# A state space scan in one long Trainium2 kernel: decays from spread running sums in the short format

## The reference, as far as it matters

```
a_cs  = cumsum(dt * A)                              # running sums, 128 tokens
decay[l, s] = exp(a_cs[l] - a_cs[s]) for l >= s, else 0
y_diag[l]   = sum_s (C[l] . B[s]) * decay[l, s] * x[s] * dt[s]
state_new   = state * exp(a_cs[last]) + sum_l B[l] * exp(a_cs[last] - a_cs[l]) * x[l] * dt[l]
y_off[l]    = (C[l] . state) * exp(a_cs[l])
y = (y_diag + y_off + d_skip * x) * silu(z)
```

## Time and profile before

| what | us |
|---|---|
| median of three runs | 2659.7 |
| span of the profiled execution | 2655.9 |
| TensorE busy | 2315.8 |
| vector engine busy | 1566.5 |
| GpSimd busy | 1499.5 |
| ScalarE busy | 716.4 |

### The profile page before, as it was taken

The page is one execution under the profiler, slowest core; times in us unless marked ns, Lnnn a source line. Parts: engine busy times, 40 slices in busy tenths (PEclk is TensorE's granted clock), DMA queues, the critical chain, the costliest instruction groups (busy, mean ns, idle before and its releaser), DMA issues.

```text
span 2655.9 us, 28354 instructions
## 1 busy us (share of the span) xinstructions
PE 2315.8 (87%) x9216; PEld 1516.6 (57%) x9216; DVE 1566.5 (59%) x3390; ACT 716.4 (27%) x1940; POOL 1499.5 (56%) x1060
## 2 busy tenths in 40 slices
PE   8999999999999999698889888898777777777776
PEld 7888778788878879586754444443233222222222
DVE  1266791434430678622388888887788776555555
ACT  2111552215421240523232222212223222111112
POOL 6777477676467763373655655655544454334331
PEclk9999999999999999899999999999999999999999
DMA  4222002222322210031399999999999999999996
GB/s 148 88 100 97 16 15 90 96 96 81 104 80 95 95 48 1 9 111 40 120 378 421 421 421 421 420 415 420 421 422 422 421 421 422 421 422 421 422 421 253
DMA packets 105898, 646.35 MB, mean 243 GB/s; under 512 B 12720, under 2 KB 15152, under 8 KB 39600
## 3 DMA queue, kind: packets, MB, share of 16 engines
q0 software_dynamic: 73728, 536.90, 48.7%
q1 hardware_dynamic: 31776, 106.87, 11.7%
q10 hardware_dynamic: 272, 1.05, 0.1%
HBM read 640.58 MB, written 4.19 MB: 243 GB/s over the span
## 4 chain that ended last, share of the span: by engine, by line
DMA 32%; PE 11%; DVE 5%; POOL 2%; issue 1%; ACT 1%; POOLq 0%; DVEq 0%; ACTq 0%
DMA peer_row<-in_peer_uv,peer_ids 32%; PE bank L3332 8%; DVE peer_row L3277 2%; PE bank L2837 1%; PE bank L2997 1%; POOL peer_row L3254 1%; ACT peer_diag L3311 1%; DVE peer_weight L3269 1%; POOL w_parts L232 1%; POOL w_parts L228 0%; PE bank L2959 0%; DVE peer_top_i L2681 0%; DVE peer_place L2681 0%; DVE peer_sc_left L2684 0%; DVE peer_top_v L2677 0%
## 5 line engine op out<-in xcount | busy, mean ns | idle before, releaser
L3332 PE MATMUL bank<-peer_row,peer_diag 128*128 128x512 f32 x2048 | 968.6, 619 | 256.9 <-ACT peer_diag L3311 255.5
L3254 POOL DMA_INDIRECT peer_row<-in_peer_uv,peer_ids x512 | 584.9, 1142 | 650.7 <-PE bank L3332 613.2
L3332 PEld LDWEIGHTS bank<-peer_row,peer_diag 128*128 128x128 f32 x2048 | 382.0, 195 | 812.5 <-ACT peer_diag L3311 416.0
L3277 DVE CUSTOM_DVE_ANT_0 peer_row<-peer_row,peer_h_tok 128x1024 f32<-128x1024 f32 x512 | 646.1, 1267 | 327.5 <-DMA peer_row<-in_peer_uv,peer_ids 326.8
L209 POOL TENSOR_TENSOR w_parts<-ring,zero 128x1024 fp32r<-128x1024 f32 x148 | 280.2, 1893 | 193.3 <-PE bank L260 84.4
L212 POOL TENSOR_TENSOR w_parts<-ring,w_parts 128x1024 fp32r<-128x1024 f32 x148 | 354.4, 2395 | 27.7 <-POOL w_parts L209 27.7
L3315 ACT ACTIVATE peer_acts<-peer_dots 128x2 f32<-128x2 f32 x256 | 52.1, 203 | 740.5 <-DVE peer_dots L3277 740.4
L3311 ACT ACTIVATE peer_diag<-ident,peer_weight 128x128 f32<-128x128 f32 x512 | 177.4, 394 | 220.7 <-DVE peer_weight L3269 220.4
L260 PE MATMUL bank<-ssm_h_high,w_parts 128*128 128x512 f32 x512 | 158.0, 389 | 0.8 <-DVEq L645 0.8
L260 PEld LDWEIGHTS bank<-ssm_h_high,w_parts 128*128 128x128 f32 x512 | 96.1, 188 | 21.1 <-DVEq L645 1.0
L284 PE MATMUL bank<-w_parts,att_h_high 128*128 128x512 f32 x320 | 98.8, 390 | 1.6 <-DVE att_h_low L445 1.6
(11 more groups left out here) (571 smaller groups left out, 3815.3 us busy)
## 6 DMA issues: line engine op xcount, KB each, us to landing
ring<-in_weights SPq DMA_DIRECT2D x180, 512.0 KB, 3.2
peer_row<-in_peer_uv,peer_ids POOLq DMA_INDIRECT x512, 24.2
resid<-in_x SPq DMA_DIRECT2D x4, 512.0 KB, 6.2
out<-resid SPq DMA_DIRECT2D x4, 512.0 KB, 7.8
xa_mem<-in_mem ACTq DMA_DIRECT2D x1, 1024.0 KB, 5.0
xa_kept<-xa_v_out SPq DMA_DIRECT2D x1, 1024.0 KB, 6.0
xa_kept<-xa_k_out SPq DMA_DIRECT2D x1, 1024.0 KB, 3.8
xa_v<-xa_kept SPq DMA_DIRECT2D x1, 1024.0 KB, 4.8
```

Source lines behind the costliest of these rows:

```text
L3254: pool.indirect_dma_start(self.rows[row][:, :], None, self.m.ins["peer_uv"], bass.IndirectOffsetOnAxis(ap=self.choice.ids[:, t, slot:slot ...
L3277: dot = dve.tensor_tensor_reduce(mine, mine, self.tokens(slot_of(j)[0]), 1.0, 0.0, ALU.mult, ALU.add, self.dots[:, h % 4, r:r + 1])
L3332: mm = pe.matmul(self.m.banks[2 * t + half][:, :], self.diag[:, j % (2 * GROUP), :], self.rows[row][:, D + half * 512:D + (half + 1) * 512 ...
```

## The change

The exponent a_cs[l] - a_cs[s] is now made from running sums that have been computed once. In the first block the sums of all heads are copied twice side by side (`twice`), transposed to rows (64 partitions: 32 heads twice, bank 7), and split into a high part in the short format F32R and the remainder (`halves`). GpSimd spreads them: row (h) holds the sums of head h in the column block h mod 4 and zero in the others (`spread_sums`). A 64 x 128 selection matrix per group (`chosen`) then sums high and low of the right heads. In the scan, TensorE adds two F32R matmuls into one bank (always bank 0): a unit matrix times the mask (`not_yet`, 0 or -2^100), and `chosen` times `spread_sums`. ScalarE takes four exponentials out of the bank with -a_cs[s] as a bias column, into SBUF. The cuts and the mask product on the vector engine are gone; `mix` multiplies the decays from SBUF with the C·B product out of its bank. y now lags by two units on TensorE and by three on the vector engine; x * dt and x * dt_end go round a ring of eight units; the banks are dealt out anew. The spreads of chunks 0 and 1 are in the first block, those of 2 and 3 in the scan's GpSimd queue at units 1 and 3.

```diff
+spread_sums = m.at(conved_kb, "ssm_sum_spread", [2 * HEADS, TT, HPG, P], F32R)
+chosen = m.at(conved_kb + 8, "ssm_chosen", [2 * HEADS, GROUPS, P], F32R)
+halves = sb("ssm_sum_halves", [2 * HEADS, TT, P], F32R)
...
+eye = sb("ssm_eye", [P, P], F32R)
+not_yet = sb("ssm_not_yet", [P, HPG, P], F32R)
...
+NEVER = -(2.0 ** 100)
+
+def spread_sum(pool, ch):
+
+    return pool.tensor_tensor(spread_sums[:, ch, :, :], again(halves[:, ch, :], HPG), spread(of_residue[:, :], P), ALU.mult)
...
-    SUMS_AFTER, EXPS_AFTER = 13, 15
-    turn_banks = [m.banks[n] for n in (0, 1, 2, 3, 5, 6, 7)]
+    SUMS_AFTER, EXPS_AFTER, SUMS_TURN_AFTER = 13, 15, 15
+    turn_banks = [m.banks[n] for n in (0, 1, 2, 3, 5, 6)]
+    sums_bank = m.banks[7]
...
+            if j == SUMS_TURN_AFTER:
+                pe.wait_ge(twice_made, 1)
+                for t in range(TT):
+                    mm = pe.transpose(sums_bank[0:2 * HEADS, t * P:(t + 1) * P],
+                                      twice[:, t, :, :].rearrange("p x h -> p (x h)"), m.ident[:, :])
+                mm.then_inc(sums_turned, 1)
+
+    @block.gpsimd
+    def _(pool):
+        pool.tensor_copy(eye[:, :], m.ident[:, :])
+        pool.tensor_scalar(not_yet[:, :, :], again(m.after[:, :], HPG), NEVER, None, ALU.mult)
+        pool.wait_ge(masks_made, 1)
+        pool.wait_ge(turned, TT + 2)
+        pool.tensor_copy(chosen[:, :, :], spread(of_group[:, 2, :], P))
+        pool.wait_ge(halves_made, 1)
+        for ch in range(2):
+            spread_sum(pool, ch)
...
+        dve.tensor_reduce(of_residue[:, :], ident.rearrange("p (m r) -> p r m", r=HPG), AX.X, ALU.add)
+        step(dve.tensor_reduce(of_group[:, 0:2, :].rearrange("p x g -> p (x g)"), ident.rearrange("p (n r) -> p n r", r=HPG),
+                               AX.X, ALU.add))
+        dve.tensor_tensor(of_group[:, 2, :], of_group[:, 0, :], of_group[:, 1, :], ALU.add).then_inc(masks_made, 1)
...
-        copies(7, N_TURN - 4)
+        copies(7, 13)
+        dve.wait_ge(pe_dt, 1)
+        sums = m.banks[4][:, 0:P].rearrange("p (t o h) -> p t o h", t=TT, o=1).broadcast_to([P, TT, 2, HEADS])
+        dve.tensor_copy(twice[:, :, :, :], sums).then_inc(twice_made, 1)
+        copies(13, 17)
+        dve.wait_ge(sums_turned, 1)
+        dve.tensor_copy(halves[:, :, :].rearrange("p t l -> p (t l)"), sums_bank[0:2 * HEADS, :]).then_inc(high_made, 1)
+        copies(17, 19)
+        low = halves[HEADS:, :, :].rearrange("p t l -> p (t l)")
+        dve.wait_ge(high_made, 1)
+        dve.tensor_tensor(low, sums_bank[HEADS:2 * HEADS, :], low, ALU.subtract).then_inc(halves_made, 1)
+        copies(19, N_TURN - 4)
...
-        act.wait_ge(pe_dt, 1)
+        act.wait_ge(twice_made, 1)
...
-        act.activation(tmp[:, 1, :], m.banks[4][:, 0:P], ACT.Copy).then_inc(act_dt, 1)
+        act.activation(flat(sum_neg), m.banks[4][:, 0:P], ACT.Copy, scale=-1.0).then_inc(act_dt, 1)
...
-x_dt = conved[:, 0:8, :].rearrange("p (b a) n -> p b (a n)", b=2)
-x_end = conved[:, 8:16, :].rearrange("p (b a) n -> p b (a n)", b=2)
-cut = sb("ssm_cut", [P, 2, HPG, P])
-cb_low = sb("ssm_cb_low", [P, 2, P])
+RING_X = GROUPS
+x_dt, x_end = (conved[:, n:n + 4, :].rearrange("p a n -> p (a n)").rearrange("p (u w) -> p u w", w=GW) for n in (8, 12))
+decay = sb("ssm_decay", [P, 2, HPG, P])
...
-LEAD = 2
+LEAD = 3
+Y_LAG, FINAL_LAG = 2, 3
...
+    seg_bank = m.banks[0]
+    cb_bank = lambda i: m.banks[1 + i % 2][:, 0:P]
+    y_bank = lambda i: m.banks[3 + i % 3][:, 0:GW]
+    new_bank = lambda i: m.banks[3 + i % 3][:, GW:]
+    old_bank = lambda i: m.banks[6 + i % 2][:, 0:GW]
...
-            if ch >= 2:
-                pool.wait_ge(y_done, i - 2 * GROUPS + 1)
+            if i >= RING_X:
+                pool.wait_ge(y_done, i - RING_X + 1)
...
         for i in range(N):
             if i + LEAD < N:
                 prepare(i + LEAD)
+            if i in (1, 3):
+                spread_sum(pool, 2 + i // 2).then_inc(spread_ready, 1)
             fade_state(i)
...
-        for i in range(N + 1):
+        for i in range(N + Y_LAG):
             if i < N:
                 ch, g = units[i]
-                pe.wait_ge(cut_ready, i + 1)
+                if i >= 1:
+                    pe.wait_ge(decay_ready, i)
+                if g == 0 and ch >= 2:
+                    pe.wait_ge(spread_ready, ch - 1)
+
+                pe.matmul(seg_bank[:, :], eye[:, :], not_yet[:, :, :].rearrange("p r l -> p (r l)"), start=True, stop=False)
+                pe.matmul(seg_bank[:, :], chosen[:, g, :], spread_sums[:, ch, :, :].rearrange("p r l -> p (r l)"),
+                          start=False, stop=True).then_inc(seg_done, 1)
+                at = slice(ch * P, (ch + 1) * P)
                 if i >= 2:
                     pe.wait_ge(mix_ready, i - 1)
...
+                pe.matmul(cb_bank(i), b_tiles[:, g, at], c_tiles[:, g, at], start=True, stop=True).then_inc(cb_done, 1)
+            if i >= Y_LAG:
+                j = i - Y_LAG
                 ch, g = units[j]
                 at = slice(ch * P, (ch + 1) * P)
...
                 pe.wait_ge(mix_ready, j + 1)
                 pe.wait_ge(x_ready, 2 * j + 2)
...
+                if j >= 3:
+                    pe.wait_ge(y_read, j - 2)
+                    pe.wait_ge(state_ready, j - 2)
+                if ch > 0:
+                    pe.wait_ge(state_ready, j - GROUPS + 1)
                 for r in range(HPG):
...
+                    pe.matmul(y_bank(j)[:, r * HD:(r + 1) * HD], mix[:, j % 2, r, :],
+                              x_dt[:, j % RING_X, r * HD:(r + 1) * HD], start=True, stop=True)
                 if ch > 0:
 
-                    pe.matmul(yb[:, GW:2 * GW], c_tiles[:, g, at], state[:, g, :], start=True, stop=True)
-                pe.matmul(sbk[:, 0:GW], b_tok[:, ch, g * STATE:(g + 1) * STATE],
-                          x_end[:, ch % 2, g * GW:(g + 1) * GW], start=True, stop=True).then_inc(y_done, 1)
+                    if j >= GROUPS + 2:
+                        pe.wait_ge(old_weighed, j - GROUPS - 1)
+                    pe.matmul(old_bank(j), c_tiles[:, g, at], state[:, g, :], start=True, stop=True)
+                pe.matmul(new_bank(j), b_tok[:, ch, g * STATE:(g + 1) * STATE], x_end[:, j % RING_X, :],
+                          start=True, stop=True).then_inc(y_done, 1)
...
+            if i < N:
+                ch, g = units[i]
+                act.wait_ge(seg_done, i + 1)
+                if i >= 2:
+                    act.wait_ge(mix_ready, i - 1)
+                for r in range(HPG):
+                    h = g * HPG + r
+                    last = act.activation(decay[:, i % 2, r, :], seg_bank[:, r * P:(r + 1) * P], ACT.Exp,
+                                          bias=sum_neg[:, ch, h:h + 1])
+                last.then_inc(decay_ready, 1)
...
+        for i in range(N + FINAL_LAG):
+            f = i - FINAL_LAG
+            if f >= 0:
+                ch, g = units[f]
+                y = y_bank(f)
+                dve.wait_ge(y_done, f + 1)
+                if ch > 0:
+                    dve.tensor_tensor(heads(part[:, f % 2, :]), heads(old_bank(f)), per_head(group(grow[:, ch, :], g), HPG), ALU.mult)\
+                       .then_inc(old_weighed, 1)
+                dve.wait_ge(skip_ready, f + 1)
+                dve.tensor_tensor(y, y, xs[:, ch, wide(g)], ALU.add).then_inc(skip_added, 1)
             if i < N:
+                dve.wait_ge(decay_ready, i + 1)
                 dve.wait_ge(cb_done, i + 1)
-                step(dve.tensor_tensor(cb_low[:, i % 2, :], m.banks[2 + i % 2][:, 0:P], m.upto[:, :], ALU.mult))
-                dve.wait_ge(decay_ready, i + 1)
                 if i >= 2:
                     dve.wait_ge(y_done, i - 1)
-                dve.tensor_tensor(mix[:, i % 2, :, :], m.banks[i % 2][:, :].rearrange("p (h l) -> p h l", h=HPG),
...
+                dve.tensor_tensor(mix[:, i % 2, :, :], decay[:, i % 2, :, :], again(cb_bank(i), HPG), ALU.mult).then_inc(mix_ready, 1)
+            if f >= 0:
+                dve.wait_ge(skip_added, f + 1)
                 if ch > 0:
-                    dve.tensor_tensor(heads(old), heads(yb[:, GW:2 * GW]), per_head(group(grow[:, ch, :], g), HPG), ALU.mult)\
-                       .then_inc(old_weighed, 1)
...
+                    dve.wait_ge(old_weighed, f - GROUPS + 1)
+                    dve.tensor_tensor(y, y, part[:, f % 2, :], ALU.add).then_inc(old_added, 1)
...
-                    dve.tensor_copy(state[:, g, :], sbk[:, 0:GW]).then_inc(state_ready, 1)
+                    dve.tensor_copy(state[:, g, :], new_bank(f)).then_inc(state_ready, 1)
...
+                    dve.wait_ge(faded, f - GROUPS + 1)
+                    dve.tensor_tensor(state[:, g, :], state[:, g, :], new_bank(f), ALU.add).then_inc(state_ready, 1)
+                    dve.wait_ge(old_added, f - GROUPS + 1)
                 gated = z_gate[:, ch, wide(g)]
                 dve.tensor_tensor(gated, gated, y, ALU.mult).then_inc(y_read, 1)
-        m.keep(step)
```

(58 more changed lines are left out.)

27 lines of the change are left out of this document (9 added, 18 removed).

## The result

The changed kernel has a median of **2684.93 us** in four runs (2683.58 to 2689.79) against 2660.61 for the kernel before in the same comparison (2659.52 to 2666.25, four runs). The ratio is 1.0089, with a 95% interval from 1.0072 to 1.0107. The forecast was 2649.2 and its range ended at 2655.5: the forecast had the wrong sign and was off by 36 us.

The account below looks back on a forecast made before the run. TensorE was taken to set the scan's pace at 2.84 us per unit. Scan -11.9, block before +1.4 and clock 0 gave 2645.4; plus 3.8 from profiled span to median, 2649.2 us, range 2646.0 to 2655.5.

Parts of the forecast that it names:

- 0.86 becomes 0.44: Decay sums on TensorE in each scan unit: two short-format matmuls at 0.22 each, 0.42 us less per unit.
- at worst the 0.43 of today: Upper bound for each of the two short-format decay-sum matmuls on TensorE, expected at 0.22 us each.
- rival F: Decay sums in the scan: the short-format pair still runs at 0.43 each, unit stays 2.84, time 2661.4 us; chance 0.02.
- Clock. I take 0, with -0.5 to +1.5 as bounds: TensorE's idle gap after the scan grows to about 4 us; half clock already paid, so no cost.
- a head of 4.34: Scan's start until first y: first units run at the pace of the ScalarE loop, y lags by two; 4.34 us.
- Rival D: Scan and block before: handshakes cost more and the clock falls in the head's gaps; +5.8, 2655 us; chance 0.09.
- The last step: After the scan: what follows starts when its last instruction ends, so a microsecond saved there is one saved overall.
- The block before: Block of transposes ahead of the scan: added work, ending with GpSimd's spreads, costs +1.4 us, bounds 0 and +2.8.
- ScalarE: four exponentials: Each scan unit: four 128-wide exponentials with a bias column, read from the bank, take 1.14 us.
- The tail: Scan's end on the vector engine, three units behind: 7.4 us, with finals 29, 30 and 31 at 1.82 each.
- Rival E: Scan: the vector product reading decays from SBUF blocks GpSimd, whose unit becomes 3.09; +9.3, 2669 us; chance 0.05.
- Rival B: Later scan chunks: GpSimd takes over the pace, its unit 2.53 if the fade waits; 2652 us; chance 0.13.

Follow-up runs that it names:

- variant 6: variant 4 with the sums' matmul reading only 64 of its 128 rows and a second such matmul right behind it: 2674.33 us, ratio 1.0052.
- variant 2: The changed kernel with TensorE's pauses ahead of and inside the scan's head filled by matmuls whose result nobody reads: 2663.63 us, ratio 1.0017.
- variant 1: The changed kernel with the decay sums laid out over 128 partitions instead of 64, the selection's upper rows zero: 2654.32 us, ratio 0.9982.
- variant 4: The changed kernel with both the sums over 128 partitions and TensorE's pauses filled: 2651.90 us, ratio 0.9971.
- variant 10: variant 4 with chunk 1's spread moved from the first block to GpSimd's queue in the scan: 2653.54 us, ratio 0.9981.
- variants 3: The changed kernel with one more full-format 256-column matmul, result not read, in each first-chunk unit: 2677.77 us, ratio 1.0073.
- variant 8: The changed kernel with only the pause ahead of the scan shortened by two full-format matmuls: 2683.05 us, ratio 1.0088.
- variant 7: The changed kernel with only the pauses between the scan's first units filled, by four short matmuls each: 2670.50 us.

## Why the prediction was wrong

**The decay sums, "0.86 becomes 0.44": the first step that failed.** "The contraction of the second is over 64 partitions; the columns count, so I take no less time" was half right: the load of 64 rows takes 0.18 where 128 take 0.19, and a matmul more of this kind adds 0.23 (variant 6). What was missing is the change of row count before and behind it, 0.39 per unit; the time of 0.44 became 0.83. The upper bound "at worst the 0.43 of today" was the truth, by another mechanism than rival F's, which had 0.02; F's time, 2661.4, is near what variant 2 gives with the clock held (2663.6). The row that I priced with, 90 matmuls in 20 us, holds only matmuls over 128 partitions and could not show it. Over the scan this is 8 x (2.40 - 1.94) + 21 x (2.83 - 2.42) = 12.3 us.

**"Clock. I take 0, with -0.5 to +1.5 as bounds": the second, and beside the first the dearer.** I looked at the gap after the scan and not at its head. My own sum had the warning in it: three times 0.66 of TensorE's work in a head of 4.34, behind a block whose end waits 2 us for GpSimd's spreads. Rival D named it, "the clock falls in the longer gaps of the head", and priced it at 1.5; it cost: in the head, (305.56 - 302.81) - (302.81 - 300.69) = 0.6 and about 0.9 more to the first y (2.03 from 305.56 to 307.59, against 1.18 in variant 2); 8 x (4.43 - 2.40) = 16.2; 1.8 in the ninth unit. Together 19.5. Most of this is not the clock's alone. The two errors met: in variant 1 the clock fell just the same, but with all loads covered it was back in 7 us (303.1 to 309.9), and its fall cost some 3 us instead of 19. Had the step on the sums been right, the change would have come out at about 2654, inside the range, with the error in the clock hidden in it. Why the uncovered loads kept the clock down for so long isn't shown.

The scan's length, by steps, from its first matmul to its last instruction's end (head to first y, units, tail):

| | forecast | changed kernel | variant 4 |
|---|---|---|---|
| head | 4.34 | 6.90 | 4.69 |
| units of first chunk | 8 x 1.94 | 8 x 4.43 | 8 x 2.01 |
| 21 later units | 50.82 | 61.28 | 51.39 |
| last units and tail | 9.16 | 9.11 | 9.11 |
| scan | 79.8 | 112.8 | 81.3 |

Once both causes are taken away, in variant 4, the sum of the scan stands to within 1.5 us. The last step held there too: the next block begins 7.9 us earlier than before, and the median is 7.0 lower. Point by point, in the changed kernel:

- The block before: its end came at 300.69 - 299.11 = **1.6** later, forecast 1.4; GpSimd's two spreads of 1.03 set it, nearly as said. They end at 299.99, and the vector engine's last product, of 128x128 with both operands in SBUF, at 300.14: beside a spread it took 0.83, and 0.28 before the change and in variant 10, where no spread runs beside it. The sum had no such wait.
- ScalarE: four exponentials in **1.14**, as the earlier trace rows had it.
- The tail: the finals alone are 1.79 apart (forecast 1.82), TensorE stands still for 3.49 after the scan (forecast about 4).
- Rival E, GpSimd blocked by the product: it holds **0.61** next to it. E falls, for a product with one operand in a bank; two engines do get in each other's way where both operands lie in SBUF, as the line on the block before shows.
- Rival B, GpSimd's pace: at 2.45 per unit in variants 1 and 4, the windows have it busy 19.37 of 20.00 against the vector engine's 19.27. It was near, but TensorE still set the pace.
- What was to show it wrong, a distance above 2.5 between the small matmuls, did.

## What to carry to other kernels

A matmul over fewer partitions than its neighbours isn't free because its columns are few: look whether its weight load, and the next one's, starts under the matmul before or with its own. Where it doesn't, padding to the neighbours' rows with zero weights is faster; here 0.39 us per unit.

A change that makes TensorE's work shorter and leaves it waiting for another engine between bursts must be priced at both clocks: first the pauses at the head of a stage, then how long the clock stays down behind them; it was 44, 10 and 7 us in three versions of the same chunk (the changed kernel, variants 3 and 1). The busy column doesn't tell it (34.00 of 34.00 at 0.50); the granted clock does. Ten matmuls whose result nobody reads, placed in the pauses, were worth 19 us beside the uncovered loads and some 3 without them.

Two causes found in one kernel are to be tried alone and together: the worth of each depended here on whether the other was there.

## What I had not expected of the hardware

A pause of 0.81 us took the clock down, behind one of 2.38 (changed kernel) and behind one of 0.66 (variant 8); a pause of 2.35 in the kernel before, and of 2.38 in variant 7's profiled run, with TensorE 1.96 and 2.00 of 2.00 busy in the window behind them, didn't. The Trainium skill ("TensorE: Matmul & The Clock Gate", section "A second HAM failure mode: psum-queue depth-cycling") tells of small idle times between groups of matmuls that make the clock go up and down; the trace agrees as to the fall, but here it stayed down, for 44 us, through a first chunk that holds the full clock when it begins with it (variant 2). What exactly the chip asks for before it gives the clock back wasn't measured. The runs of variants 3 and 7 differ by up to 11 us among themselves; how much of that is the clock in the scan and how much scatter behind it is open.
